# A transformer layer's output projection as three float32r products, and a ring of six tiles in its final combination

## What is computed

```python
mod = (silu(c) @ w_ada + b_ada)                 # shift, scale, gate, twice
...
mix = concatenate([rmsnorm(attn, attn_out_g), ssm * norm_g], -1) @ w_out
h   = x + gate1 * mix
n2  = rmsnorm(h, norm2_g) * (1 + scale2) + shift2
...                                             # router, experts
ffn = w_a * y_a + w_b * y_b                     # each token's two experts
out = rmsnorm(h + gate2 * ffn, final_g)
```

## Time and profile before

| | us |
|---|---|
| runs, median of 3 | 3632.66 (3630.17 to 3637.58) |
| the profiled execution, its own time | 3630.65 |
| its span, first to last instruction | 3628.8 |
| PE busy | 2977.3 (82%) |
| DVE busy | 2391.4 (66%) |
| ACT busy | 1554.2 (43%) |
| POOL busy | 558.5 (15%) |
| products of the output projection (L1498), 576 passes | 255.7 |
| mean granted TensorE clock | 0.914 |

### The profile page before, as it was taken

One profiled execution on the slowest core, in us unless ns is written; L12 is line 12 of the kernel. 1 busy time (PEld: TensorE's weight loads), 2 busy tenths in 40 slices (PEclk: granted clock), 3 DMA queues, 4 the chain that ended last, 5 costly groups with the idle time before them and its releaser, 6 DMA issues. The chain is left out here.

```text
span 3628.8 us, 41802 instructions
## 1 busy us (share of the span) xinstructions
PE 2977.3 (82%) x12653; PEld 1939.6 (53%) x12653; DVE 2391.4 (66%) x2967; ACT 1554.2 (43%) x1752; POOL 558.5 (15%) x413
## 2 busy tenths in 40 slices
PE   6999999489999999967783799819999999999920
PEld 3666666334444444434442455407777777777720
DVE  2555555347777777748996344347887888887855
ACT  2323332013333333343221122107788777777743
POOL 0000000000000000006660000042222222222224
PEclk8999999669999999988985899859999999999965
DMA  6112121521011110120005233345577776568347
GB/s 241 47 38 66 46 54 42 171 41 33 21 35 35 32 34 20 29 87 1 0 0 190 96 120 117 113 174 188 211 255 265 289 264 234 203 249 313 114 169 275
DMA packets 238793, 445.74 MB, mean 123 GB/s; under 512 B 22658, under 2 KB 96478, under 8 KB 237966
## 3 DMA queue, kind: packets, MB, share of 16 engines
q1 hardware_dynamic: 222141, 397.16, 32.6%
q0 software_dynamic: 16592, 47.84, 3.7%
HBM read 366.93 MB, written 86.40 MB: 125 GB/s over the span
## 5 line engine op out<-in xcount | busy, mean ns | idle before, releaser
L2090 DVE TENSOR_TENSOR weights_rest<-w,weights_rounded 128x2048 fp32r<-128x2048 f32 x314 | 716.3, 2289 | 191.8 <-ACT weights_rounded L2025 191.7
L2025 ACT ACTIVATE weights_rounded<-w 128x2048 fp32r x314 | 598.4, 1913 | 148.6 <-PE ps_up L1949 93.8
L823 ACT ACTIVATE probs<-ps_scores 128x1024 f32<-128x1024 f32 x260 | 266.1, 1023 | 503.8 <-PE ps_scores L754 442.0
L846 DVE TENSOR_REDUCE part_max<-ps_max 128x1 f32<-128x512 f32 (+1 forms) x528 | 338.0, 678 | 193.8 <-PE ps_max L731 193.7
L1949 PE MATMUL ps_up<-weights_rounded,block_T_rounded 128*128 128x512 f32 x832 | 339.6, 408 | 28.5 <-DVE weights_rest L2090 24.0
L430 PE MATMUL ps_proj<-w_in,n1T 128*128 128x512 f32 (+2 forms) x1152 | 348.0, 460 | 6.5 <-PEq L108 6.5
L1949 PE MATMUL ps_up<-weights_rounded,block_T_rest 128*128 128x512 f32 x832 | 327.4, 394 | 0.0
L1949 PE MATMUL ps_up<-weights_rest,block_T_rounded 128*128 128x512 f32 x832 | 326.1, 392 | 0.0
L764 PE MATMUL ps_attn<-probs,v 128*64 128x512 f32 x1040 | 283.7, 625 | 0.0
L430 PEld LDWEIGHTS ps_proj<-w_in,n1T 128*128 128x128 f32 x1152 | 197.8, 193 | 144.9 <-issue 130.0
L1498 PE MATMUL ps_out<-x_and_B,mix_T 128*128 128x512 f32 x576 | 255.7, 603 | 11.2 <-DVE mix_T L1539 11.2
(11 more groups left out here) (335 smaller groups left out, 4695.4 us busy)
## 6 DMA issues: line engine op xcount, KB each, us to landing
w<-in_w SPq DMA_DIRECT2D x96, 2048.0 KB, 10.7
expert_rows<-scratch_y SPq DMA_DIRECT2D x36, 512.0 KB, 5.0
w_ada_rest<-in_w_ada SPq DMA_DIRECT2D x5, 2048.0 KB, 16.0
scratch_qT<-qT_stage SPq DMA_DIRECT2D x18, 512.0 KB, 3.5
q_for_max<-scratch_qT SPq DMA_DIRECT2D x36, 256.0 KB, 5.7
q_rounded_twice<-scratch_qT SPq DMA_DIRECT2D x36, 256.0 KB, 4.3
mix_rows<-scratch_mix SPq DMA_DIRECT2D x18, 512.0 KB, 4.3
scratch_h<-h_rows SPq DMA_DIRECT2D x18, 512.0 KB, 2.6
```

Source lines behind the costliest of these rows:

```text
L823: act.activation(pf[:, slot(p, n), :], ps_s[:, n % 2, :], ACT.Exp).then_inc(exp_done, 1)
L846: nc.vector.tensor_reduce(mx[:, p, n // H, n % H:n % H + 1], ps_m[:, n % 2, 0:PART], AX.X, ALU.max).then_inc(m_taken, 1)
L2025: act.activation(split_piece(wh, s), raw_piece(s, buf[0]), ACT.Copy).then_inc(hi_done, 1)
L2090: nc.vector.tensor_tensor(split_piece(wl, s), raw_piece(s, buf), split_piece(wh, s).bitcast(F32), ALU.subtract).then_inc(lo_done, 1)
```

## The change

In `output_phase` the gain moves ahead of the transposes: two new loads bring the gains of all 1024 columns as a row (`gains`), and `norm_mix` multiplies by the reciprocal and by the gain in one instruction. The transposed tile is then split in two by a new ScalarE step, `round_mT`, which copies it out of PSUM rounded to float32r (`mTh`), and a new VectorE step, `rest_mT`, which subtracts that from PSUM (`mTl`). The weights are split in the same way, once, into `wh` and `wl`, slice by slice, ScalarE behind tile 0's `round_mT`, VectorE behind tile 1's `norm_mix`. A product becomes three: `mTh` with `wh`, `mTh` with `wl`, `mTl` with `wh`. Tile 0 keeps the plain product (`project_first`), from a copy in unused columns of `x_and_B`. `norm_mix(0)` goes ahead of VectorE's wait for the constants.

In `combine_phase` loads, expert rows and output rows get six buffers (`RING`), SP runs five tiles ahead, all 18 tiles are written out as plain code, and the weights are read where they lie.

```diff
+            for name, at in (("attn_out_g", 0), ("ssm_norm_g", 512)):
+                sp.dma_start(gains[:, at:at + 512], rows_of(I[name], P, 512)).then_inc(gains_in, 16)
             sp.dma_start(g2[:, :], rows_of(I["norm2_g"], P, D)).then_inc(consts_in, 16)
...
+            def round_mT(t, p):
+                act.wait_ge(m_turned, t + 1)
+                wait(act, o_ready, t - 1)
+                dst = mT_first[:, :, :] if isinstance(t, int) and t == 0 else mTh[:, p]
+                act.activation(dst, ps_m[:, :, :], ACT.Copy).then_inc(mTh_ready, 1)
             mix_rms(0, 0)
+            round_mT(0, 0)
+            act.wait_ge(S["w_out_loaded"], 16)
+            for k in range(KC):
+                act.activation(wh[:, k, :], w[:, k, :], ACT.Copy).then_inc(wh_ready, 1)
             for t, p in query_tiles(act, NT):
                 own.at(1 + t * 2)
                 if not is_last(t):
                     mix_rms(t + 1, 1 - p)
+                    round_mT(t + 1, 1 - p)
...
             def project(t, p):
-                pe.wait_ge(mT_ready, t + 1)
+                pe.wait_ge(mTh_ready, t + 1)
+                pe.wait_ge(mTl_ready, t)
+                if isinstance(t, int) and t == 1:
+                    pe.wait_ge(wh_ready, KC)
+                    pe.wait_ge(wl_ready, KC)
                 wait(pe, o_taken, t)
                 for n in range(2):
                     for k in range(KC):
-                        last = nc.tensor.matmul(ps_o[:, n * 512:(n + 1) * 512], mT[:, p, k, :], w[:, k, n * 512:(n + 1) * 512],
-                                                start=(k == 0), stop=(k == KC - 1))
+                        cols = slice(n * 512, (n + 1) * 512)
+                        nc.tensor.matmul(ps_o[:, cols], mTh[:, p, k, :], wh[:, k, cols], start=(k == 0), stop=False)
+                        nc.tensor.matmul(ps_o[:, cols], mTh[:, p, k, :], wl[:, k, cols], start=False, stop=False)
+                        last = nc.tensor.matmul(ps_o[:, cols], mTl[:, p, k, :], wh[:, k, cols], start=False, stop=(k == KC - 1))
...
-                    last = nc.vector.tensor_scalar(m[:, p, a:b], m[:, p, a:b], st[:, p, 2, n:n + 1], None, ALU.mult)
+                    last = nc.vector.scalar_tensor_tensor(m[:, p, a:b], m[:, p, a:b], st[:, p, 2, n:n + 1], gains[:, a:b], ALU.mult, ALU.mult)
...
-            def gain_mix(t, p):
-                dve.wait_ge(m_turned, t + 1)
-                gains = S["cols"][:, 68:76].rearrange("p (k o) -> p k o", o=1).to_broadcast([P, KC, P])
-                nc.vector.tensor_tensor(mT[:, p], ps_m[:, :, :], gains, ALU.mult).then_inc(mT_ready, 1)
+            def rest_mT(t, p):
+                dve.wait_ge(mTh_ready, t + 1)
+                nc.vector.tensor_tensor(mTl[:, p], ps_m[:, :, :], mTh[:, p].bitcast(F32), ALU.subtract).then_inc(mTl_ready, 1)
...
+            dve.wait_ge(gains_in, 32)
+            norm_mix(0, 0)
             dve.wait_ge(consts_in, 16 * 14)
...
                     norm_mix(t + 1, 1 - p)
+                if isinstance(t, int) and t == 0:
+                    for k in range(KC):
+                        dve.wait_ge(wh_ready, k + 1)
+                        nc.vector.tensor_tensor(wl[:, k, :], w[:, k, :], wh[:, k, :].bitcast(F32), ALU.subtract).then_inc(wl_ready, 1)
                 residual(t, p, group(t))
                 if not is_last(t):
-                    gain_mix(t + 1, 1 - p)
+                    rest_mT(t + 1, 1 - p)
```

And in the combination, SP's part:

```diff
-            def load(t, p, turn):
-                wait_alone(sp, gated, t - 2, S["passed"])
+            def load(t):
+                wait(sp, gated, t - RING + 1)
                 for k in range(2):
...
-                wait_alone(sp, res_ready, t - 2, S["passed"])
+                wait(sp, res_ready, t - RING + 1)
...
-            load(1, 1, 0)
-            for t, p, turn in tiles_by_three(sp):
-                if at := ahead(t, p, turn, 2):
-                    load(*at)
-                wait_alone(sp, o_ready, t + 1, S["passed"])
+            for t in range(1, RING - 1):
+                load(t)
+            for t in range(NT):
+                if t + RING - 1 < NT:
+                    load(t + RING - 1)
+                sp.wait_ge(o_ready, t + 1)
```

More of the change, by code:

```diff
@@ L1491, in turn_n2, with project_first @@
                 last.then_inc(n_turned, 1)
-            def project(t, p):
-                pe.wait_ge(mT_ready, t + 1)
+            def project_first():
+                pe.wait_ge(mTh_ready, 1)
+                for n in range(2):
+                    for k in range(KC):
+                        last = nc.tensor.matmul(ps_o[:, n * 512:(n + 1) * 512], mT_first[:, k, :], w[:, k, n * 512:(n + 1) * 512],
+                                                start=(k == 0), stop=(k == KC - 1))
+                last.then_inc(o_ready, 1)
+            def project(t, p):
+                pe.wait_ge(mTh_ready, t + 1)
[3 more added lines that the diff above has]
+                    pe.wait_ge(wl_ready, KC)
                 wait(pe, o_taken, t)
@@ L1513, in _ @@
                 first = isinstance(t, int) and t == 0
-                project(t, p)
+                if first:
+                    project_first()
+                else:
+                    project(t, p)
                 if not first:
@@ L2216, in _ @@
             gp.wait_ge(consts_in, 48)
-            for t, p, turn in tiles_by_three(gp):
-                wait_alone(gp, summed, t + 1, S["passed"])
-                wait_alone(gp, res_ready, t - 2, S["passed"])
-                gp.tensor_tensor(yg[:, p, :], y[:, p, 1, :], gate[:, group(t), :], ALU.mult).then_inc(gated, 1)
+            for t in range(NT):
+                gp.wait_ge(summed, t + 1)
+                wait(gp, res_ready, t - 2)
+                gp.tensor_tensor(yg[:, t % 3, :], y[:, t % RING, 1, :], gate[:, group(t), :], ALU.mult).then_inc(gated, 1)
         @block.scalar
@@ L2240, in _ @@
         @block.vector
         def _(dve):
-            def weights(t, p, turn):
-                wait(dve, summed, t - 2)
-                dve_w = S["weights"][:, :, bass.ds(t, 1)].rearrange("p k o -> p (k o)")
-                nc.vector.tensor_scalar(ws[:, p, :], dve_w, 1.0, None, ALU.mult).then_inc(ws_ready, 1)
-            def add_rows(t, p, turn):
-                dve.wait_ge(a_ready, t + 1)
-                nc.vector.scalar_tensor_tensor(y[:, p, 1, :], y[:, p, 1, :], ws[:, p, 1:2], y[:, p, 0, :], ALU.mult, ALU.add).then_inc(summed, 1)
@@ L2251, in _, with add_rows @@
-            dve.wait_ge(consts_in, 48)
-            weights(0, 0, 0)
-            weights(1, 1, 0)
-            add_rows(0, 0, 0)
-            for t, p, turn in tiles_by_three(dve):
-                if at := ahead(t, p, turn, 2):
-                    weights(*at)
-                if at := ahead(t, p, turn, 1):
-                    add_rows(*at)
-                dve.wait_ge(gated, t + 1)
-                dve.wait_ge(h_in[p], turn * 16 + 16)
-                wait(dve, stored[p], turn * 16)
-                nc.vector.tensor_tensor(o[:, p, :], yg[:, p, :], h[:, p, :], ALU.add).then_inc(res_ready, 1)
+            def add_rows(t):
+                dve.wait_ge(a_ready, t + 1)
+                nc.vector.scalar_tensor_tensor(y[:, t % RING, 1, :], y[:, t % RING, 1, :], S["weights"][:, 1, t:t + 1], y[:, t % RING, 0, :],
+                                               ALU.mult, ALU.add).then_inc(summed, 1)
@@ L2264, in _ @@
+            add_rows(0)
+            for t in range(NT):
+                if t + 1 < NT:
+                    add_rows(t + 1)
+                dve.wait_ge(gated, t + 1)
+                dve.wait_ge(h_in[t % RING], 16 * turn(t))
+                wait(dve, stored[t % RING], 16 * (t // RING))
+                nc.vector.tensor_tensor(o[:, t % RING, :], yg[:, t % 3, :], h[:, t % RING, :], ALU.add).then_inc(res_ready, 1)
+                if t == 0:
+                    dve.wait_ge(consts_in, 48)
                 dve.wait_ge(st_ready, t + 1)
-                nc.vector.reciprocal(st[:, p, 2:3], st[:, p, 1:2]).then_inc(inv_ready, 1)
+                nc.vector.reciprocal(st[:, t % 3, 2:3], st[:, t % 3, 1:2]).then_inc(inv_ready, 1)
```

86 lines of the change are left out of this document (40 added, 46 removed).

## The result

The changed kernel takes 3593.24 us (median of 4 runs, 3591.17 to 3595.93) beside 3635.12 for the kernel before in the same runs (3630.17 to 3638.28). The ratio is 0.9886, 95% interval [0.9869, 0.9904]: faster by 1.1%. The forecast was 3581, the range 3567 to 3597. The profiled execution took 3591.17 us with a span of 3589.3.

A forecast was written before the change was run, and what follows sets the result against it. The load chain was to bound projection tiles, VectorE the combination. From 3630.65 us, minus 29 (projection) and 21 (combination) gave 3580.6, predicted as 3581; own bounds 3571 to 3592, range with neighbouring rivals 3567 to 3597.

The forecast's parts named there:

- Combination, 21 us: Final combination: six buffers bring rows in time, turns fall from 6.78 to 5.62 us, last residual add 3600.2 against 3621.47.
- The reason given for 5.62: Combination turn: VectorE's own need, 1.20 us for the sum of rows plus 4.42 to the next residual add.
- DMA bounds the combination: Rival, combination: at 350 GB/s a tile takes 5.98 us; lead worth nothing, 6 us go, 3587; chance 0.13.
- the load chain: Projection, steady tiles: scaling, transposes, rounding, norm, store, load and squares in sequence bound a tile; sum 16.05, used 16.1 us.
- The slack of 2.5 us: Projection before the change: transposes could start at 2169.8, while TensorE comes free at 2172.3.
- The scaling: Projection, VectorE's scaling with a gain row: 1.45 us, between 1.0 and 2.0; the ends move the total 7 us.
- thirteen turns of 16.1: Projection, from tile 3's reciprocal at 2061.8: load-chain turns bring tile 16's reciprocal to 2271.1.
- the clock falls once in each tile: Rival, projection: TensorE idles 1.6 us a turn, a fall costs 1.7, turn 16.9, 12 us go, 3593; chance 0.07.
- The start: Projection, first tiles: transposes at about 2006.5 instead of 2009.26, product 1 at 2033.8 against 2032.23, tile 3's reciprocal at 2061.8.
- no shorter: Rival, projection: products bound by weight loads, 18.1 us a tile, only the combination gains, 3615; chance 0.05.
- slower: Rival, projection: products never see the full clock, 26.1 us a tile instead of 17.8, 3750; chance 0.04.
- TensorE bounds the projection: Rival: store and load quicker by a microsecond, 15.2 us a tile, 14 us more gained, 3567; chance 0.09.

The follow-up runs named there:

- two products: Changed kernel with each tile's third product (`mTl` with `wh`) left out, 32 products a tile instead of 48; ratio 0.9865 to the kernel before.
- gaps filled: Changed kernel with three unused products in each of TensorE's two pauses of a turn, before the mix-row transposes and before the product; ratio 0.9869 to the kernel before.
- early loads: Changed kernel with SyncE asking for mix rows of tile t+2 once tile t is transposed, ahead of the `n2` store; ratio 0.9855 to the kernel before.

## Why the prediction was right where it was, and what failed

**Combination, 21 us: right in every number, by a reason that was half right.** Start to first residual add 16.47 us (forecast 16.6), first turn 6.70 (6.6), then 5.62 (5.62), last residual add 111.9 us after the first load (112.0). The reason given for 5.62 was half right. I called it what VectorE itself needs; it is VectorE and GpSimd by turns, and the 1.5 us of ScalarE's root in it lie beside the gating. The row I took it from, a turn of the kernel before without a late load, held the same chain, so the number came out right without the reason for it. *DMA bounds the combination* fell: DMA moved 416 GB/s in the window above, more than the 350 that I had worked out of the earlier trace rows, ran ahead of the engines and left ScalarE without late rows. The 358 GB/s that the Trainium skill (DMA: Bandwidth & Descriptors, Specifications) gives for a core were no bound here either, where the kernel runs on one core.

**Projection: the load chain was right, the turn of 16.1 held only where the clock did not fall.** The slack of 2.5 us read from the kernel before left out the 1.04 us of `n2` transposes that TensorE does first; no term of the sum rests on it. The floor is 16.04 us (two products) and 16.10 (gaps filled); TensorE's own turn is 15.33 (forecast 15.2). The scaling, taken at 1.45 between 1.0 and 2.0, measured 1.54, the estimate by the Trainium skill's page (VectorE: DVE Perf Modes). The step that failed is the term "thirteen turns of 16.1", in which every product had the full clock: 7 of 16 products ran 3.4 us at a granted 0.50. The rival *the clock falls once in each tile* had the size right (a fall costs 1.6 us and gives a turn of 16.9; forecast 1.7 and 16.9), and was judged as all or nothing, where falls came in 7 of 16 tiles here and in 9 and 14 in two other runs of the same code. From tile 3's reciprocal to tile 17's this made 16.56 - 16.1 = 0.46 us a turn, 14 x 0.46 = 6.5 us. That the measured 3593.24 is that rival's own figure of 3593 is chance: only 6.5 of its 12 us were falls. The time lies above the forecast's own bounds (3571 to 3592) and inside the stated range because the range took in the neighbouring rivals.

**The start, mis-sized by 1.8 us.** Tile 3's reciprocal came 79.1 us after the first load instead of 77.3. The constants came 2.2 us later, not 0.95 (23.2 against 21.0 from first load to VectorE's sight of them): the two new loads took the 0.95 us to issue, and the constants behind them 1.3 us more than before. Part of it was made good behind them: product 1 is 0.8 us late, and ran 13.8 us instead of 12.8. Product 2 was a long one as well, but tile 3's reciprocal came 1.7 us ahead of its end and not, as in the forecast, with it, so this fall adds nothing here.

6.5 + 1.8 = 8.3 of the 8.7 us. The remaining 2 us to the forecast of the profiled execution lie ahead of the change: SyncE's first load in this stage stood at 1986.62, before at 1984.49. The median lies another 2.1 us above that execution; the forecast had read 2.0 for this from the kernel before and left it out of its 3581. The other rivals fell: products cost 11.17 us and not 13.8, so neither *no shorter* nor *slower* came; *TensorE bounds the projection* holds only once the loads go out early.

## What to carry to other kernels

When a shorter product uncovers a chain of loads, sum the chain link by link as here, then move the load off it: asking a turn earlier brought 15 us, the falls that went with it included, and transposes put inside the product a further 19. A forecast for a TensorE stage that gets a new pause should price a share of falls in the clock, and not none or all: here 7, 9 and 14 of 16 products in three executions of the same code, 1.6 us each on the product, of which 0.8 reached the turn (16.9 against 16.1), as the load chain had covered the rest. Before an engine's share of a turn is called its own work, look for a neighbour that lengthens its instructions: an operation of 1.28 us that shows 3.18 beside GpSimd is a wait.

## What the runs showed that was not expected

- A pause of 0.7 us in front of the product went with long products in one run (9 of 15) and with none in another (early loads), with the same pause and the same product; the falls also came seven in a row and then stopped, and three executions of the same projection code had 7, 14 and 9 of them.
- Falls vanished when the pause in front of the product was filled, while one of up to 0.8 us in front of the transposes did not matter; after waits of 1.9 to 4.0 us there, in the run with two products, they came without a pause in front of the product.
- Final scaling on VectorE took 3.18 us beside GpSimd's gating and 1.28 without it, with the residual add beside the head of the same gating unchanged at 1.21.
